# Gate columns of two layers: from one full-width group of products to four column groups of the array with a summing product

## The reference, cut to what matters

```
ba = (the 16 gate columns of a @ w_in)
beta = sigmoid(ba[:, :, 0])
g = -exp(a_log) * softplus(ba[:, :, 1] + dt_bias)
```

```
proj = x @ w_in
qk = proj[..., :2 * MLSTM_QK_W]
...
gates = proj[..., 2 * MLSTM_QK_W + 2 * D_MODEL:].astype(jnp.float32) + gate_b.astype(jnp.float32)
qk = jax.nn.silu(_causal_conv(qk, conv_w).astype(jnp.float32))
...
log_i = gates[..., :MLSTM_HEADS]
log_f = jax.nn.log_sigmoid(gates[..., MLSTM_HEADS:])
```

## Time and profile before

| what | us |
|---|---|
| median of three runs | 2289.66 |
| the profiled execution's own time | 2289.95 |
| its span, first to last instruction | 2288.1 |
| TensorE busy | 2221.1 (97%) |
| VectorE busy | 1617.5 (71%) |
| ScalarE busy | 1156.7 (51%) |

### The profile page before, as it was taken

The page is one execution under the profiler, slowest core; times in us unless marked ns, Lnnn a source line. Parts: engine busy times, 40 slices in busy tenths (PEclk is TensorE's granted clock), DMA queues, the critical chain, the costliest instruction groups (busy, mean ns, idle before and its releaser), DMA issues.

```text
span 2288.1 us, 41418 instructions
## 1 busy us (share of the span) xinstructions
PE 2221.1 (97%) x17332; PEld 2045.9 (89%) x17332; DVE 1617.5 (71%) x2749; ACT 1156.7 (51%) x1937; POOL 150.9 (7%) x142
## 2 busy tenths in 40 slices
PE   7999999999999999999999999999999999999998
PEld 3665979998879999999999989997779999999998
DVE  4398667655977655798557787577988557799654
ACT  3425355443365446756345664345556345957343
POOL 0013000000000000000000000015630000000000
PEclk9999999999999999999999999999999999999999
DMA  8248054555244554414554425552024554514552
GB/s 365 74 198 318 25 215 167 186 185 201 93 166 166 185 185 167 182 56 178 182 182 161 147 93 203 184 221 74 19 94 184 184 184 169 183 54 166 185 184 74
DMA packets 50873, 368.46 MB, mean 161 GB/s; under 512 B 5632, under 2 KB 5888, under 8 KB 6528
## 3 DMA queue, kind: packets, MB, share of 16 engines
q1 hardware_dynamic: 50544, 363.72, 43.1%
q10 hardware_dynamic: 144, 2.10, 0.2%
HBM read 364.75 MB, written 1.05 MB: 160 GB/s over the span
## 4 chain that ended last, share of the span: by engine, by line
PE 81%; DVE 11%; ACT 5%; issue 2%; DMA 0%; SPq 0%; DVEq 0%; POOL 0%; ACTq 0%
PE psum L268 67%; DVE weight_rest L262 2%; PE psum L4515 1%; PE psum L3076 1%; PE psum L4516 1%; ACT weight_parts L226 1%; PE psum L4537 1%; PE psum L3710 1%; PE psum L2726 1%; DVE work L2028 1%; PE psum L4551 1%; DVE work L3540 1%; DVE spare L2516 0%; DVE work L2515 0%; DMA weight_ring<-stream_dram 0%
## 5 line engine op out<-in xcount | busy, mean ns | idle before, releaser
L268 PE MATMUL psum<-input_parts,weight_parts 128*128 128x256 f32 x5184 | 931.6, 283 | 6.4 <-DVE work L1495 1.8
L268 PEld LDWEIGHTS psum<-input_parts,weight_parts 128*128 128x128 f32 x5184 | 799.3, 189 | 11.6 <-issue 5.7
L268 PE MATMUL psum<-input_parts,weight_rest 128*128 128x256 f32 x2592 | 732.6, 283 | 0.0
L262 DVE TENSOR_TENSOR weight_rest<-weight_ring,weight_parts 128x1024 fp32r<-128x1024 f32 x528 | 619.9, 1220 | 149.3 <-ACT weight_parts L226 148.9
L226 ACT ACTIVATE weight_parts<-weight_ring 128x1024 fp32r<-128x1024 f32 x540 | 538.0, 1051 | 122.5 <-PE psum L268 121.7
L268 PEld LDWEIGHTS psum<-input_parts,weight_rest 128*128 128x128 f32 x2592 | 487.8, 188 | 0.0
L268 PE MATMUL psum<-hidden_parts,weight_parts 128*128 128x256 f32 x2496 | 450.8, 283 | 2.6 <-DVE weight_rest L262 1.3
L268 PEld LDWEIGHTS psum<-hidden_parts,weight_parts 128*128 128x128 f32 x2496 | 385.0, 189 | 5.9 <-issue 3.4
L268 PE MATMUL psum<-hidden_parts,weight_rest 128*128 128x256 f32 x1248 | 352.1, 282 | 0.0
L268 PEld LDWEIGHTS psum<-hidden_parts,weight_rest 128*128 128x128 f32 x1248 | 234.9, 188 | 0.0
L1479 ACT ACTIVATE work<-psum 128x256 f32<-128x256 f32 x118 | 45.3, 384 | 352.4 <-PE psum L268 350.0
(11 more groups left out here) (532 smaller groups left out, 2855.9 us busy)
## 6 DMA issues: line engine op xcount, KB each, us to landing
weight_ring<-stream_dram SPq DMA_DIRECT2D x340, 1024.0 KB, 4.8
constants<-constants_dram SPq DMA_DIRECT2D x1, 2304.0 KB, 17.1
work<-s_bc_dram ACTq DMA_DIRECT2D x1, 2048.0 KB, 9.7
work<-ctx_dram SPq DMA_DIRECT2D x1, 1024.0 KB, 5.3
residual<-x_dram SPq DMA_DIRECT2D x1, 1024.0 KB, 7.3
work<-first_dram SPq DMA_DIRECT2D x1, 1024.0 KB, 14.9
out_dram<-residual SPq DMA_DIRECT2D x4, 256.0 KB, 2.1
vectors<-vectors_dram SPq DMA_DIRECT2D x1, 486.5 KB, 14.3
```

Source lines behind the costliest of these rows:

```text
L262: ins = dve.tensor_tensor(self.rest[:, i % RING, cols], self.ring[:, i % RING, cols], self.parts[:, s % SPLITS, cols].bitcast(F32), ALU.su ...
L268: mm = pe.matmul(*args, **kw)
```

## The change

The gate weights of both layers are laid out so that feature chunk c has its 16 gate columns (8 and 8) side by side. Each of the 8 products now has 32 stationary columns (its own 16 and the next 16, which nobody reads) and writes to one of four 32-row strips of the bank, at strip c % 4, so that products 0 to 3 start the four strips and 4 to 7 add to them. ScalarE copies all 128 rows of partial sums to SBUF, and one product with a constant selection matrix of 72 columns (`gate_sum`) adds the four strips and puts the two kinds of gates in rows 0 to 7 and 64 to 71 of the same bank. The instructions that read the gates then wait for this product.

In the hybrid layer the copy stands on ScalarE behind the square of head 2 and ahead of the roots of heads 0 and 1, and the summing product on TensorE behind chunk 5, ahead of sum 2. In the mLSTM layer the copy stands on ScalarE at n = 1 where the five gate instructions were; those move to n = 2, behind the bias of raw job 1 and ahead of the silu of chunk 0; the summing product stands on TensorE between slabs 2 and 3. The late part of the constants, one DMA of 2304 KB, grows by 36 KB, and the scratch that the program sets aside for dynamic DMAs goes from 1024 to 64.

```diff
+def gate_strips(k, pe, out, name, x, ready=None):
+    for c in range(KC):
+        at = STRIP * (c % 4)
+        if ready:
+            pe.wait_ge(*ready[c])
+        mm = pe.matmul(out[at:at + STRIP, :], k.v(name, 16 * c, STRIP), x[:, c, :], start=(c < 4), stop=(c >= 4),
+                       tile_position=(0, at))
+    return mm
...
 class HybridProjection: tensor
+            if n == 5:
+                self.sum_gates(pe)
             for i in self.sums_after.get(n, ()):
                 self.sum_head(pe, i)
...
     def gates(self, pe):
-        rows = KC * 8 + 8
-        w = self.k.v("hyb_g_w", 0, 2 * KC * 8)
-        for c in range(KC):
-            mm = pe.matmul(job.ap[0:rows, 0:T2], w[:, 8 * c:8 * c + rows], self.a[:, c, :],
-                           start=(c == 0), stop=(c == KC - 1))
-        mm.then_inc(job.full[0], 1)
+        gate_strips(self.k, pe, job.ap[:, 0:T2], "hyb_gates_w", self.a).then_inc(job.full[0], 1)
+
+    def sum_gates(self, pe):
+        pe.wait_ge(*self.gate_copied)
+        pe.matmul(self.gate_job.ap[0:GATE_ROWS, 0:T2], self.k.c("gate_sum"), self.gate_strips, start=True, stop=True)\
+          .then_inc(self.gate_summed[0], 1)
...
             for i in self.sums_after.get(n + 1, ()):
                 self.square(act, i)
+            if n == 4:
+                act.wait_ge(*self.gate_job.full)
+                act.activation(self.gate_strips, self.gate_job.ap[:, 0:T2], ACT.Identity)\
+                   .then_inc(self.gate_copied[0], 1)
             if n == 5:
                 self.gate_exps(act)
...
     def gate_exps(self, act):
-        act.wait_ge(*job.full)
+        act.wait_ge(*self.gate_summed)
...
 class MlstmIn: tensor
-        project_columns(k, pe, x, self.jobs[2:4])
+        project_columns(k, pe, x, self.jobs[2:3])
+        self.sum_gates(pe)
+        project_columns(k, pe, x, self.jobs[3:4])
...
             if n == 1:
                 act.wait_ge(*self.gate_job.full)
+                act.activation(self.gate_strips, self.gate_job.ap[:, 0:T], ACT.Identity)\
+                   .then_inc(self.gate_copied[0], 1)
+            if n == 2:
+                act.wait_ge(*self.gate_summed)
                 act.activation(r[0:8, 0, :], self.gate_job.ap[0:8, 0:T], ACT.Identity, bias=k.v("mlstm_gate_i", rows=8))
```

More of the change, by code:

```diff
@@ L65 @@
 ROUND = 12582912.0
+GATE_ROWS = 72
 VECTORS = [
@@ L71 @@
     ("hyb_conv_w", CONV_A * 12), ("hyb_out_norm", 1), ("hyb_q_norm", 1), ("hyb_k_norm", 1),
-    ("hyb_a_log", 1), ("hyb_dt_bias", 1), ("hyb_g_w", KC * 8), ("hyb_beta_w", KC * 8),
+    ("hyb_a_log", 1), ("hyb_dt_bias", 1), ("hyb_gates_w", KC * 16),
     ("conf_b_in", 2 * KC), ("conf_dw_w", CONV_C * KC), ("conf_dw_b", KC),
@@ L76 @@
     ("mlstm_conv_w", CONV_M * KC), ("mlstm_gate_i", 1), ("mlstm_gate_f", 1), ("mlstm_norm_w", KC),
-    ("mlstm_i_w", KC * 8), ("mlstm_f_w", KC * 8),
+    ("mlstm_gates_w", KC * 16),
     ("s5_a_re", S5_TILES), ("s5_a_im", S5_TILES), ("s5_log_dt", S5_TILES), ("s5_d", KC),
@@ L84 @@
     ("cos", T), ("sin", T), ("head_rows", HEADS * P),
-    ("time", T), ("future", 2 * P),
+    ("time", T), ("future", 2 * P), ("gate_sum", GATE_ROWS),
 ]
@@ L1758, in setup @@
         self.conv_ready = k.counter("conv_ready").events(12)
-        self.gate_taken, self.gate_exp = k.counter("gate_taken").events(2)
+        self.gate_copied, self.gate_taken, self.gate_exp = k.counter("gate_taken").events(3)
+        self.gate_strips = k.area(H_GATE + 2 * T2, T2)
         self.gates_ready = self.columns.gates_ready
@@ L1779, in setup @@
             if n == 4:
+                self.gate_summed = k.bank_full[k.jobs % BANKS]
                 self.gate_job = k.job(self.gate_taken)
+                self.gate_summed = self.gate_summed.event()
             for i in self.sums_after.get(n, ()):
@@ L3894, in setup @@
         self.rows = k.area(L_ROWS, 8, T)
-        self.gate_taken = k.counter("mlstm_gate_taken").event()
+        self.gate_copied, self.gate_taken = k.counter("mlstm_gate_taken").events(2)
         self.qk_taken = k.counter("mixer_q").events(4)
@@ L3902, in setup @@
         self.jobs = [k.job_in_two_banks(e) for e in self.qk_taken[0:2]]
+        self.gate_summed = k.bank_full[k.jobs % BANKS]
         self.gate_job = k.job(self.gate_taken)
+        self.gate_summed = self.gate_summed.event()
+        self.gate_strips = self.o[:, 0, :]
         self.jobs += [k.job(e) for e in self.qk_taken[2:] + self.v_ready + self.o_ready]
@@ L3936, in gates, with sum_gates @@
         begin(pe, self.gate_job)
[L3937 to L3943, removed]
+        gate_strips(k, pe, self.gate_job.ap[:, 0:T], "mlstm_gates_w", k.h, self.h_ready)\
+            .then_inc(self.gate_job.full[0], 1)
+    def sum_gates(self, pe):
+        pe.wait_ge(*self.gate_copied)
+        pe.matmul(self.gate_job.ap[0:GATE_ROWS, 0:T], self.k.c("gate_sum"), self.gate_strips, start=True, stop=True)\
+          .then_inc(self.gate_summed[0], 1)
     def scalar(self, act):
@@ L4895, in small, with both @@
         return np.asarray(w).reshape(KC, P, 8).transpose(1, 0, 2).reshape(P, KC * 8)
+    def both(a, b):
+        return np.stack([a.reshape(P, KC, 8), b.reshape(P, KC, 8)], 2).reshape(P, KC * 16)
     def states(a):
@@ L4905, in pack_vectors @@
     v["hyb_a_log"], v["hyb_dt_bias"] = rows(i["hyb_a_log"]), rows(i["hyb_dt_bias"])
-    v["hyb_beta_w"], v["hyb_g_w"] = small(i["hyb_w_in"][0][:, 2048:2056]), small(i["hyb_w_in"][0][:, 2056:2064])
+    v["hyb_gates_w"] = both(small(i["hyb_w_in"][0][:, 2056:2064]), small(i["hyb_w_in"][0][:, 2048:2056]))
     v["hgrn_norm_w"] = chunks(i["hgrn_norm_w_2"])
@@ L4911, in pack_vectors @@
     v["mlstm_norm_w"] = chunks(i["mlstm_norm_w_2"])
-    v["mlstm_i_w"], v["mlstm_f_w"] = (small(i["mlstm_w_in_2"][0][:, 3072 + 8 * j:3080 + 8 * j]) for j in range(2))
+    v["mlstm_gates_w"] = both(*(small(i["mlstm_w_in_2"][0][:, 3072 + 8 * j:3080 + 8 * j]) for j in range(2)))
     v["s5_a_re"], v["s5_a_im"] = states(i["s5_a_re_2"]), states(i["s5_a_im_2"])
@@ L4966, in pack_constants @@
     c["future"] = np.concatenate([np.where(t[:, None] <= t[None, :], 0.0, FUTURE), np.zeros((P, P))], 1)
+    c["gate_sum"] = np.zeros((P, GATE_ROWS))
+    for r in range(8):
+        c["gate_sum"][r::STRIP, r] = c["gate_sum"][8 + r::STRIP, 64 + r] = 1.0
     for name, size in CONSTANTS:
@@ L4994 @@
     arrays = launch_arrays(inputs, ORDER)
-    nc = _bacc.Bacc("TRN2", target_bir_lowering=False, num_devices=1, dynamic_dma_scratch_size=1024)
+    nc = _bacc.Bacc("TRN2", target_bir_lowering=False, num_devices=1, dynamic_dma_scratch_size=64)
     build(nc, arrays, ORDER)
```

## The result

| kernel | median us | range | ratio to before, 95% interval |
|---|---|---|---|
| before | 2289.66 | 2287.6 to 2291.8 | |
| changed | 2269.56 | 2266.74 to 2272.72 | 0.9912 (0.9898 to 0.9927) |

The forecast was 2285.5 us with a range of 2282.5 to 2288.5.

The account below looks back on a forecast made before the run. TensorE, with 81% of the chain that ended last, was taken to bound the kernel. From the profiled 2289.95 us, hybrid -5.0 and mLSTM +0.8 give 2285.75; the median being 0.29 lower, 2285.5 us, range 2282.5 to 2288.5.

Parts of the forecast that it names:

- The larger constants (36 KB beside 2304) and the smaller scratch I cost at nothing: Whole kernel: bigger constants and smaller scratch add nothing; at most some tenth of a microsecond if the transfer were on the path.
- The strips: Hybrid gate products in four column groups: 6.87 us becomes 1.87 (bounds 1.72 to 2.0), giving back 5.0 us.
- the modulation's row: Profile row of existing four-column-group work: 8 float32 products of 256 columns take 1.00 us start to start.
- The surplus of 0.14 us: Modulation's 1.00 us less 0.86 for perfect overlap of four: the unshared cost, changes of tiling shape included.
- the rival of less overlap: Gate groups, each with its own stationary data, overlap less; half the overlap lost gives hybrid gain 3.4, 2287.1 us; chance 0.1.
- The copy and the summing product in the hybrid layer: Copy (0.60 us) hidden in ScalarE's idle time, summing product (0.86 us) hidden by waiting at the transposes; full 5.0 us kept.
- The mLSTM input: TensorE alone would gain 1.4 us; late splits stall slabs 5 and 6 by 1.0 and 1.4, netting 0.8 us slower.
- the mLSTM keeps its gain: Stalls at slabs 5 and 6 don't come, so the mLSTM layer gives 1.4 us: 2283.3 us; chance 0.2.
- no overlap: Column groups don't overlap at all: hybrid gives 0, mLSTM is 1.15 us later, 2290.8 us; chance 0.04.
- a later wait: Part of the hybrid gain ends in a wait between 107.8 and 178 us, leaving 1 to 4 us: 2286.5 to 2289.5; chance 0.08.

Follow-up runs that it names:

- run 1: Kernel before with only the dynamic DMA scratch cut from 1024 to 64: 2290.07 us, ratio 0.9997.
- run 3: Changed kernel with the scratch back at 1024, so weights lie as before and inputs 288 bytes further: 2268.70 us, ratio 0.9908.
- run 2: Kernel before, old gate products, with scratch 64 and an unused 288-byte tensor behind the constants, giving the changed kernel's layout: 2272.63 us, ratio 0.9927.
- run 5: Kernel before, scratch 1024, with an unused 32-byte tensor behind the constants, moving inputs but not weights: 2274.11 us, ratio 0.9930.
- run 8: Kernel before with scratch 1056 and a 32-byte tensor behind the constants: weights 32 bytes further, inputs 64: 2274.59 us, ratio 0.9926.
- run 4: Changed kernel in exactly the old layout: scratch 1024, summing matrix in its own tensor behind all others: 2283.65 us, ratio 0.9975 to before.
- run 10: Changed kernel with mLSTM copy behind slab 4's rounding, gate instructions and silu behind slab 5's rounding, `forget` behind split 6: 2266.51 us, ratio 0.9896.
- run 9: Changed kernel with the mLSTM strip copy moved right behind the rounding of slab 4, ahead of raw job 0's ends: 2268.90 us, ratio 0.9904.

## Why the prediction was wrong, step by step

- **The sentence "The larger constants (36 KB beside 2304) and the smaller scratch I cost at nothing" is the step that failed.** It asked what they add to transfers and found nothing, which was right (run 1 with the small scratch gives 2290.07 us, and run 3 with the larger constants is as fast as the changed kernel). It didn't ask where the other tensors come to lie. Runs 2, 5 and 8 put that at 15 to 17 us without any gate change, run 4 against the changed kernel at about 14. None of the rivals had it, and no bound in the sum could have held it: all of them lay in the two stretches of the diff. In the old layout the gate change takes 2283.65 us (run 4), inside the stated range; there the forecast of 2285.5 was 1.9 us too slow.
- **The strips**: 1.87 us expected from the modulation's row, 1.86 measured from start to start. The surplus of 0.14 us for changes of tiling mode held also where the groups' stationary data differ, so the rival of less overlap is out. By the share of a perfect overlap that the Trainium skill, "TensorE: Matmul & The Clock Gate", section Why this matters for your kernels, gives for three column groups, the estimate was 2.2 us; the measured 1.86 decides. The Trainium skill, "TensorEngine Tiling (Array Packing)", section Tiling Modes, says that a change of tiling mode drains the engine; it gives no price, and here two such changes and all other overhead together take the 0.14 us.
- **The copy and the summing product in the hybrid layer** were hidden as forecast, the transposes waiting 0.88 us (75.05 less 74.17 in the forecast's sum, 0.88 too). 5.0 us were forecast for the layer and 4.8 measured, and they are still there at 276 us. What the forecast lacked is the 1.5 us of clock at 343 us.
- **The mLSTM input**: a loss of 0.8 was forecast where TensorE alone would have gained 1.4; the loss is 0.4. The mechanism is the gate instructions that stand ahead of the rounding of slab 5. The changed kernel's trace shows it (VectorE idle for 2.28 us until that rounding), run 10 takes it away together with the place of `forget` and brings 2.0 us, and run 9, which takes away only the wait for the copy, brings none. Two details were off. The prediction had the summing product "done at 1249.6, long before", while by its own line the copy that it needs began at 1250.4: that is the 1.20 us wait. And split 6 was placed to end 27.07 us behind the first gate product and ended at 26.71, 0.4 us sooner: the sum put full durations end to end at three new joints, where the trace starts the next instruction about 0.1 us ahead of the end of the one before (L1186 at 1236.66 behind a split that ends at 1236.75, the gates at 1239.31 behind a bias that ends at 1239.41). Because the wait for the copy lay ahead of the later limit, the first error cost nothing in the total; that was luck.
- **The rival "the mLSTM keeps its gain"** is refuted for this change; run 10 keeps a gain of that size (1.6 us).
- **The two slower or smaller rivals** (no overlap, a later wait) didn't happen.

The account of the 20.1 us: about 14 layout (the median of run 4 less that of the changed kernel), 4.8 the hybrid's products, 1.5 the clock behind them, less 0.4 in the mLSTM input; that sums to 20. The first is a difference of medians that carry 1 to 3 us of noise each, and other pairs of runs give 15 to 17; the other three are read from traces and make 5.9 where run 4 measures 6.3. That the sum comes out so well is in part luck.

## What to carry to other kernels

A diff that changes the size of any tensor or of the scratch moves all tensors behind it: compare the start-to-start time of untouched work in both traces before crediting the edit, and run the old code in the new layout. A group of thin float32 products (few output columns) over the same bank is worth packing into four column groups (6.87 to 1.86 us for 8 products of 512 columns) if the copy and the summing product fall into idle time that exists. When instructions are moved on an engine that also feeds another pipeline, follow that pipeline to its first due date, and if it has no slack, put them behind the feeding instruction.

## What the runs showed of the hardware that was not expected

The rate of dense split products (weights stationary, 256 moving columns) depends on where the two operands lie relative to each other in SBUF: with equal remainders modulo 64 bytes they start every 118.7 to 120.0 ns, 32 bytes apart every 117.3 ns in most stretches, 0.7% of this kernel's time. Shifts of both by 32 or by 960 bytes, or of one by 256, changed nothing (2288.7 to 2290.1 us). Also new: the granted clock fell to its lower level within 1.6 us behind single waits of 1.74 us (five traces) and 1.58 us (two), while the same wait of 1.58 us was followed by no fall in twelve of fourteen traces. What decides between the two wasn't tried.
